# Gathers that hold 64 tokens for two heads, summed through stacked 128x64 diagonals

## The reference

```python
q = (xn @ wq).reshape(t, PEER_HEADS, PEER_D_KEY)
s1, s2 = einsum(q halves, keys1 / keys2)        # 128 scores each
v1, i1 = top_k(s1, 16); v2, i2 = top_k(s2, 16)
cs, ci = top_k(v1[..., :, None] + v2[..., None, :] flattened, 16)
expert = i1[ci // 16] * 128 + i2[ci % 16]
gate = softmax(cs)
act = gelu(einsum('td,thkd->thk', x, u_tab[expert]))
out = einsum('thk,thkd->td', gate * act, v_tab[expert])
```

## Time and profile before

| what | value |
|---|---|
| time, median of 3 executions | 4200.38 us (4197.98 to 4206.7) |
| the profiled execution, its own time | 4207.45 us |
| its span, first to last instruction | 4205.5 us |
| first gather to last `dot`, experts 0 | 527.5 to 2471.3 us |
| first gather to last `dot`, experts 1 | 2886.6 to 4183.9 us |
| gathers | 1280, 1342.31 MB |
| mean granted TensorE clock | 0.95 |

### The profile page before, as it was taken

How to read it: one execution, slowest core, us unless ns; L and a number is a source line. 1 busy time by engine, 2 the same in 40 slices (tenths; PEclk the granted TensorE clock), 3 DMA queues, 4 the chain that set the end, 5 groups by cost and what they waited for, 6 DMA issues and landing times. The chain is left out here.

```text
span 4205.5 us, 32412 instructions
## 1 busy us (share of the span) xinstructions
PE 3372.7 (80%) x9736; PEld 1548.5 (37%) x9736; DVE 2633.3 (63%) x6027; ACT 1513.4 (36%) x4394; POOL 1618.9 (38%) x1482
## 2 busy tenths in 40 slices
PE   4998887888788888788777768677887877977776
PEld 0893633333233333233222237563322322322222
DVE  3314397857857866866864444437887587587444
ACT  3210143343343343343333332333434334433333
POOL 1005044544444444444444330212444444444332
PEclk7999999999999999999999989898999999999999
DMA  8117299999999999999999951006999999999998
GB/s 353 50 61 281 95 403 394 421 421 421 417 422 416 418 413 417 418 418 418 416 405 421 422 241 60 1 33 267 394 421 421 421 419 420 421 411 415 422 421 332
DMA packets 215391, 1455.21 MB, mean 346 GB/s; under 512 B 25920, under 2 KB 25920, under 8 KB 44080
## 3 DMA queue, kind: packets, MB, share of 16 engines
q0 software_dynamic: 184704, 1342.31, 77.2%
q1 hardware_dynamic: 30400, 110.72, 7.1%
q10 hardware_dynamic: 112, 0.11, 0.0%
HBM read 1447.72 MB, written 5.34 MB: 346 GB/s over the span
## 5 line engine op out<-in xcount | busy, mean ns | idle before, releaser
L1459 PE MATMUL peer_py<-peer_ring,peer_diag 128*128 128x512 f32 x5120 | 2514.5, 626 | 617.8 <-ACT peer_diag L1389 606.4
L1342 POOL DMA_INDIRECT peer_ring<-in_uv_dram,peer_idx x1280 | 1472.0, 1150 | 1803.7 <-PE peer_py L1459 1682.8
L1559 DVE CUSTOM_DVE_ANT_0 peer_ring<-peer_ring,peer_f 128x1024 f32<-128x1024 f32 x1280 | 1555.9, 1225 | 925.3 <-DMA peer_ring<-in_uv_dram,peer_idx 915.3
L1459 PEld LDWEIGHTS peer_py<-peer_ring,peer_diag 128*128 128x128 f32 x5120 | 929.1, 195 | 2155.5 <-ACT peer_diag L1389 1324.0
L1383 ACT ACTIVATE peer_gel<-peer_u 128x1 f32<-128x1 f32 x1280 | 258.8, 202 | 1833.0 <-DVE peer_u L1559 1831.6
L1389 ACT ACTIVATE peer_diag<-ident,peer_coef 128x128 f32<-128x128 f32 x1280 | 513.8, 401 | 41.7
L1387 ACT ACTIVATE peer_coef<-peer_gel,peer_gate 128x1 f32<-128x1 f32 x1280 | 377.1, 295 | 46.3
L353 DVE TENSOR_TENSOR m_w_low<-m_w_low_plain,m_w_high 128x2048 fp32r<-128x2048 f32 x26 | 61.1, 2349 | 220.6 <-ACT m_w_high L348 220.6
L361 PE MATMUL m_ps<-m_w_high,m_aT_high 128*128 128x512 f32 x416 | 166.0, 399 | 4.4 <-DVE m_v L820 1.8
L1434 PE MATMUL peer_pb<-arena,peer_fT 128*128 128x512 f32 x320 | 164.1, 610 | 2.4 <-ACT peer_fT L1356 2.4
L361 PE MATMUL m_ps<-m_w_low,m_aT_high 128*128 128x512 f32 x416 | 163.8, 394 | 0.0
(11 more groups left out here) (194 smaller groups left out, 2400.0 us busy)
## 6 DMA issues: line engine op xcount, KB each, us to landing
mod_rows_sb<-in_ada_w_dram SPq DMA_DIRECT2D x33, 1024.0 KB, 5.0
peer_ring<-in_uv_dram,peer_idx POOLq DMA_INDIRECT x1280
arena<-in_ada_w_dram SPq DMA_DIRECT2D x15, 1024.0 KB, 16.2
m_w_low_plain<-in_ev_w_in_dram SPq DMA_DIRECT2D x12, 1024.0 KB, 5.1
arena<-in_peer_wq_dram SPq DMA_DIRECT2D x2, 4096.0 KB, 19.2
mod_rows_sb<-mod_rows SPq DMA_DIRECT2D x7, 1024.0 KB, 7.1
m_w_low_plain<-in_od_w_in_dram SPq DMA_DIRECT2D x6, 1024.0 KB, 5.2
m_w_low_plain<-in_ev_w_out_dram SPq DMA_DIRECT2D x4, 1024.0 KB, 5.1
```

Source lines behind the costliest of these rows:

```text
L1342: pool.indirect_dma_start(ring[:, n % RING], None, A["uv"], bass.IndirectOffsetOnAxis(idx[:, i % 2, hd, k:k + 1], 0)).then_inc(sem(f"lande ...
L1459: ins = pe.matmul(PY[:, i % 2, b], diag[:, n % RING], ring[:, n % RING, D + b * HALF:D + (b + 1) * HALF], start=s == 0, stop=s == TS - 1)
L1559: dve.tensor_tensor_reduce(x, x, f[:, i % 2], 1.0, 0.0, ALU.mult, ALU.add, u[:, n % RING:n % RING + 1]).then_inc(sem("dot"), 1)
```

## The change

Two slots now share two heads. Slot s belongs to pair s // 32, place s // 2 % 16 and g = s % 2, the half of the tile's tokens. Its gather brings, on partitions 0 to 63, the rows that 64 tokens (half g) have at the pair's first head, and on partitions 64 to 127 those that the same 64 tokens have at its second head. The number of gathers and their bytes are the same. For that the token rows, the indices and the gates must lie so that partition p and p + 64 hold the same token:

- `modulate` writes `plain`; ScalarE copies the half that stays (`f_kept`, at slot 14) and SyncE moves the other half (`rows_moved`) into `f[:, i % 2, g]`. `plain` also takes the place of `y`.
- SyncE moves indices (`places_moved`) and gates (`gates_moved`) by four DMAs each for a pair of heads or a batch (`spread`), one for each half of the tokens and each head of the pair. GpSimd waits for `idx_moved`, ScalarE for `gate_moved`.
- The diagonal is `stacked` times the coefficient: two 64x64 identities one above the other, 128x64. A matmul with it adds the two heads of a token. Half g = 0 goes to PSUM partitions 0 to 63, half g = 1 to 64 to 127, and `combine` takes two slots at a time, at every odd slot.
- The batches of the first tile's gates are (0,2), (2,4), (4,8) in place of (0,2), (2,5), (5,8).
- VectorE's chained waits in all stages use one semaphore; the instructions are the same. GpSimd makes `stacked` in the modulation stage (three instructions).

```diff
+def unit_of(s):
+    return s // 2 // TOPK, s // 2 % TOPK, s % 2
...
-        diag = sb("diag", [P, RING, P])
+        diag = sb("diag", [P, RING, HALF_P])
...
         @block.sync
+            def spread(i, to, of, lo, hi, name):
+                by_pair = of[:].rearrange("p (h x) k -> p h x k", x=2)
+                for g in range(2):
+                    for x in range(2):
+                        sp.dma_start(to[x * HALF_P:(x + 1) * HALF_P, i % 2, g, lo:hi],
+                                     by_pair[g * HALF_P:(g + 1) * HALF_P, lo:hi, x]).then_inc(sem(name), 16)
+            def rows_moved(i):
+                sp.wait_ge(sem("f"), i + 1)
...
+                for g in range(2):
+                    sp.dma_start(f[(1 - g) * HALF_P:(2 - g) * HALF_P, i % 2, g], plain[g * HALF_P:(g + 1) * HALF_P]
+                                 ).then_inc(sem("f_moved"), 16)
+            def places_moved(i, pair):
+                sp.wait_ge(sem("idx"), i * NH + 2 * pair + 2)
...
+                if i * PAIRS + pair:
+                    sp.wait_ge(sem("idx_moved"), MOVES * (i * PAIRS + pair))
+                spread(i, idx_at, idx, pair, pair + 1, "idx_moved")
+            def gates_moved(i, b):
+                lo, hi = gates_of(i)[b]
+                sp.wait_ge(sem("gate"), batch_ready(i, lo))
...
+                spread(i, gate_at, gate, lo // 2, hi // 2, "gate_moved")
+            for i in range(first, last + 1):
+                rows_moved(i)
+                for pair in range(PAIRS):
+                    places_moved(i, pair)
+                    for b, (lo, hi) in enumerate(gates_of(i)):
+                        if hi == 2 * pair + 2:
+                            gates_moved(i, b)
...
         @block.gpsimd
                     if k == 0:
-                        pool.wait_ge(sem("idx"), i * NH + hd + 1)
+                        pool.wait_ge(sem("idx_moved"), MOVES * (i * PAIRS + pair + 1))
                     if n >= RING:
                         pool.wait_ge(sem("slot_free"), n - RING + 1)
...
+            def f_kept(i):
+                act.wait_ge(sem("f"), i + 1)
...
+                for g in range(2):
+                    half = slice(g * HALF_P, (g + 1) * HALF_P)
+                    act.activation(f[half, i % 2, g], plain[half], ACT.Copy).then_inc(sem("f_kept"), 1)
...
-                act.activation(diag[:, n % RING], ident[:], ACT.Copy, scale=coef[:, at]).then_inc(sem("diag"), 1)
+                act.activation(diag[:, n % RING], stacked[:], ACT.Copy, scale=coef[:, at]).then_inc(sem("diag"), 1)
...
-                pe.wait_ge(sem("diag"), n + 1)
+                pe.wait_ge(sem("diag"), n + 2)
                 for b in range(2):
-                    ins = pe.matmul(PY[:, i % 2, b], diag[:, n % RING], ring[:, n % RING, D + b * HALF:D + (b + 1) * HALF],
-                                    start=s == 0, stop=s == TS - 1)
-                ins.then_inc(sem("slot_free"), 1)
+                    for g in range(2):
+                        at = (n + g) % RING
+                        ins = pe.matmul(PY[g * HALF_P:(g + 1) * HALF_P, i % 2, b], diag[:, at],
+                                        ring[:, at, D + b * HALF:D + (b + 1) * HALF], start=s == 0, stop=s == TS - 2)
+                ins.then_inc(sem("slot_free"), 2)
...
                 for s in range(TS):
-                    combine(i, s)
+                    if s % 2 == 1:
+                        combine(i, s - 1)
...
+            def plain_free(i):
+                if i > 0:
+                    dve.wait_ge(sem("fT_ps"), i)
+                    dve.wait_ge(sem("f_moved"), 32 * i)
+                    dve.wait_ge(sem("f_kept"), 2 * i)
...
+                if i > 0:
+                    dve.wait_ge(sem("idx_moved"), MOVES * ((i - 1) * PAIRS + hd // 2 + 1))
-                dve.tensor_scalar(idx[:, i % 2, hd], ef[:], float(layer * EXPERTS), None, ALU.add).then_inc(sem("idx"), 1)
+                dve.tensor_scalar(idx[:, hd], ef[:], float(layer * EXPERTS), None, ALU.add).then_inc(sem("idx"), 1)
```

More of the change, by code:

```diff
@@ L111, with group_rows @@
 GROUP_TERMS = GROUPS * TILES + 4
-def group_rows(dve, S, tag, g, row, ps, bias, gain, before):
+def group_rows(dve, S, tag, g, row, ps, bias, gain):
     for j in range(TILES):
         at = tile_rows(j)
-        dve.tensor_tensor(row[at], ps[at], bias[at, g], ALU.add).then_inc(S(tag + "_sum"), 1)
-    dve.wait_ge(S(tag + "_sum"), before + TILES)
+        linked(S, dve.tensor_tensor(row[at], ps[at], bias[at, g], ALU.add))
+    wait_links(dve, S)
     scaled = [j for j in range(TILES) if group_tile(g, j)[1] == 1]
@@ L123, in group_rows @@
         at = tile_rows(j)
-        dve.scalar_tensor_tensor(row[at], row[at], 1.0, gain[at], ALU.add, ALU.mult).then_inc(S(tag + "_sum"), 1)
-    done = before + TILES + len(scaled)
-    dve.wait_ge(S(tag + "_sum"), done)
+        linked(S, dve.scalar_tensor_tensor(row[at], row[at], 1.0, gain[at], ALU.add, ALU.mult))
+    wait_links(dve, S)
     dve.sem_inc(S(tag + "_rows"), 1)
-    return done
 def store_group(queue, mod_d, layer, g, row, sem):
@@ L1225 @@
 TS = NH * TOPK
+MOVES = 64
 PIECES = 4
@@ L1250, in next_piece, with peer_stage @@
     return None
-def peer_stage(nc, S, A, h, ident, mod_d, arena, rows, layer, t0, first, n_tiles):
+def peer_stage(nc, S, A, h, ident, stacked, mod_d, arena, rows, layer, t0, first, n_tiles):
     with ExitStack() as ctx:
@@ L1263, in peer_stage @@
         wq, keys = peer_buffers(arena)
-        f = sb("f", [P, 2, D])
+        f = sb("f", [P, 2, 2, D])
+        plain = sb("f_plain", [P, D])
         fT = sb("fT", [P, KC, P])
@@ L1283, in peer_stage @@
         ef = sb("ef", [P, TOPK])
-        idx = sb("idx", [P, 2, NH, TOPK], U32)
+        idx = sb("idx", [P, NH, TOPK], U32)
+        idx_at = sb("idx_at", [P, 2, 2, PAIRS, TOPK], U32)
         shifted = sb("shifted", [P, NH, TOPK])
@@ L1288, in peer_stage @@
         grec = sb("grec", [P, NH])
-        gate = sb("gate", [P, 2, NH, TOPK])
+        gate = sb("gate", [P, NH, TOPK])
+        gate_at = sb("gate_at", [P, 2, 2, PAIRS, TOPK])
         u = sb("u", [P, RING])
@@ L1393, in _ @@
             f_turned(first)
+            f_kept(first)
+            act.wait_ge(S("stacked"), 3)
             for part in range(2):
@@ L1408, in _ @@
                             f_turned(i + 1)
+                            f_kept(i + 1)
                         for part in range(2):
@@ L1501, in modulate @@
             def modulate(i):
-                x = f[:, i % 2]
+                x = plain[:]
                 dve.wait_ge(sem("root"), i + 1)
+                plain_free(i)
                 link(dve.reciprocal(ss[:, 3:4], ss[:, 2:3]))
@@ L1550, in normalise @@
                 link(dve.reciprocal(grec[:, lo:hi], gsum[:, lo:hi]))
-                dve.tensor_tensor(gate[:, i % 2, lo:hi], gexp[:, lo:hi],
+                if i > 0:
+                    dve.wait_ge(sem("gate_moved"), MOVES * (batch_ready(i, 0) - 1))
+                dve.tensor_tensor(gate[:, lo:hi], gexp[:, lo:hi],
                                   grec[:, lo:hi].rearrange("p (h o) -> p h o", o=1).broadcast_to([P, hi - lo, TOPK]), ALU.mult
@@ L1557, in dot @@
                 dve.wait_ge(sem(f"landed{n % RING}"), 16 * (n // RING + 1))
+                if s == 0:
+                    dve.wait_ge(sem("f_moved"), 32 * (i + 1))
+                    dve.wait_ge(sem("f_kept"), 2 * (i + 1))
                 x = ring[:, n % RING, 0:D]
[L1559 removed]
+                dve.tensor_tensor_reduce(x, x, f[:, i % 2, s % 2], 1.0, 0.0, ALU.mult, ALU.add, u[:, n % RING:n % RING + 1]).then_inc(sem("dot"), 1)
             def add_up(i):
@@ L1564, in add_up @@
                     dve.wait_ge(S("peer_gates"), 16 * rows_loads)
-                dve.tensor_tensor(y[:], PY[:, i % 2].rearrange("p b n -> p (b n)"), rows[:, kind(i - shift), 2], ALU.mult).then_inc(sem("y"), 1)
+                plain_free(min(i + 2, last + 1))
+                dve.tensor_tensor(plain[:], PY[:, i % 2].rearrange("p b n -> p (b n)"), rows[:, kind(i - shift), 2], ALU.mult).then_inc(sem("y"), 1)
                 dve.wait_ge(sem("y"), i + 1)
-                link(dve.tensor_tensor(h[:, i - shift], h[:, i - shift], y[:], ALU.add))
+                link(dve.tensor_tensor(h[:, i - shift], h[:, i - shift], plain[:], ALU.add))
             dve.wait_ge(S("peer_rows"), 16 * rows_loads)
```

87 lines of the change are left out of this document (51 added, 36 removed).

## The result

The changed kernel takes 4278.8 us (median of 4, 4267.16 to 4291.11) against 4203.54 us before: ratio 1.0178, 95% interval [1.0142, 1.0214], 75 us slower. The forecast was +58 us, with a range of its own from +30 to +83. The profiled execution is the longest of the four, with a span of 4288.8 us, 83.3 more than before.

What follows compares the result with a forecast made beforehand. The prediction took the DMA engines' gathers to bound the two expert stages. Its terms, 24.8 + 5 + 10 + 18 = 58 us on the median 4200.4, gave 4258 us, own range 4230 to 4284, stated range 4226 to 4308.

Steps and rivals of the forecast that it cites:

- The pace is set by the DMA engines: Both expert stages: they last as long as their gathers' bytes, 1280 gathers at 2.48 us, 3174 of 3241 us.
- The rival that TensorE paced the ring: Expert stages: late buffers cause 67 us and cheaper slots recover them, giving 4191 us; chance 0.05.
- the halves do not overlap: Expert stages: a pair's eight instructions take 3.6 us, the queue covers the lateness, giving 4262 us; chance 0.07.
- The start: Start of each expert stage: first gather waits for both heads and index moves, 12.4 us later, 24.8 us in all.
- Indices and gates: Index and gate moves beside gathers: about 2460 small packets a tile at 12.4 ns, 18 us over 9.5 tiles.
- each piece as dear as 512 B: Index and gate moves: 64 B pieces at 19.4 ns each would make the term about 28 us.
- The token rows: Token-row moves inside SBUF: 1.24 us a tile at the gathers' rate, 10 us for eight tiles; bounds 0 to 20.
- The hole and the pairs: First tile of each stage, near slot 42: freeing in pairs queues one gather fewer, 2.5 us a stage, 5 us.
- about five gathers queued: Gather ring: pairs free the even buffer 2.5 to 3 us later, leaving five gathers, 12 us cover, costed at nothing.
- Halves and clock: TensorE's sum for a pair: halves run together in four rounds, about 1.8 us at full clock; no gain booked.
- its rival: Expert stages: TensorE's clock falls to 1.2 GHz, costing 8 us in each of eight tiles, 64 us; chance 0.08.
- The sum: Whole kernel: start, hole, token rows, indices and gates add up to 58 us, own range 30 to 83.

Runs made afterwards that it cites:

- b_half: Kernel before, with the second matmul of each slot left out except at a tile's first and last slot; ratio 1.0012 to the kernel before.
- b_start: Kernel before, with GpSimd's first gather of a pair of heads waiting until both heads are routed; ratio 1.0032 to the kernel before.
- a_one_half: Changed kernel, with both token halves summed into the lower 64 array columns except at a tile's first and last pair; ratio 1.0206 to the kernel before.
- b_rows_one: Kernel before, plus one unread move of token rows per tile, 128 partitions in one transfer; ratio 1.0020 to the kernel before.
- b_pair: Kernel before, with the sum done for two slots at a time and both buffers freed together, diagonals still 128x128; ratio 1.0037 to the kernel before.
- b_all_moves: Kernel before, plus unread row, index and gate moves, GpSimd's wait for moved indices and buffers freed in pairs, without the 128x64 halves; ratio 1.0207 to the kernel before.
- b_rows: Kernel before, plus two unread moves of 64 token rows of 4 KB for each tile; ratio 1.0059 to the kernel before.
- b_small: Kernel before, plus the change's index and gate moves on SyncE into tiles nobody reads; ratio 1.0034 to the kernel before.

## Why the forecast held, point by point

- *The pace is set by the DMA engines.* Shown by b_half, and by b_start, where a later first gather is paid in full. The rival that TensorE paced the ring is out for the kernel before. In the changed kernel it is out only because the halves run side by side: a_one_half, with pairs of 3.65 us, is short of gathers in places (share 0.97). The prediction priced this case (*the halves do not overlap*) at under 4 us and held that the queue would cover the rest. The step of 5.4 us that it reckoned with is measured as 5.49; what failed is that the queue covers it: it cost 23 us of the phases, and 12 in the time.
- *The start*: forecast 24.8 us, measured 12.9 + 11.9 = 24.8. The moves' issues were dearer (2.38 us for four, against 1.7), so GpSimd starts 3.8 us after head 1's index is written and not 3.4; the sum is right to within what the two stages differ by. The terms that the prediction names (3.1 us behind 536.51) give 539.6 and not 539.9, so 24.2 us; that it meets the measured sum to the tenth is chance.
- *Indices and gates*: 18 us from 12.4 ns a packet; measured alone 15.4 us, 10.1 ns. The estimate that the prediction tied to the Trainium skill's statement on transfers below 512 B ("DMA: Bandwidth & Descriptors", Specifications), each piece as dear as 512 B, would have given about 28; the run speaks against so high a price for pieces of 64 B. The upper end of 25 us that the prediction's own range uses for this term is worked out nowhere, and its check of the packet count leaves 384 over (1280 gathers of 128 rows and 16 signals are 184320, not 184704).
- *The token rows*: this is the mis-sized term. Forecast 10 us from their bytes, bound 20; measured 27.5 alone. The bytes were right (b_rows_one 8.5), the step that failed was that a move costs its bytes at the gathers' rate whatever its partitions. The same page, Rules for kernel authors, advises one transfer of 128 partitions in place of two to disjoint halves, because they serialize; this case agrees with the advice and is dearer than serializing explains. That it is the halves of SBUF into which each transfer writes at one time is my reading, not shown: b_rows_one changes the number of transfers and the partitions of each together, and neither one transfer of 64 partitions nor one of 128 that crosses the halves was tried.
- *The hole and the pairs*: forecast 5 us and "about five gathers queued"; b_pair alone costs 14.3, all of it in the first tile of each stage, half of it outside the hole. The cover of five gathers, costed at nothing, held in the later tiles and not in the first; which of the first tile's waits makes the other half was not separated. In the changed kernel the hole costs 10.6 us of gathers (309 GB/s over 40 us) where it cost 6.7.
- *Halves and clock*: four rounds, 1.94 us, as forecast; the clock fell as its rival said, to a mean of 0.79, but it brought none of its 64 us: with the clock low in part of its pairs the changed kernel's phases equal, within 1 us, those of b_all_moves, whose mean clock is 0.938. The rival wanted the low clock in the query steps, and of these only the first has it: from 940 to 960 us (the row is shown with a_one_half) it is 1.00 and the DMA engines are full, as the argument against the rival had it. The low clock falls into pairs with slack around them.
- *The sum.* 24.8 + 45.4 + 1.7 = 71.9 of the 75 us. One by one the parts of the phases make 58.7; together 46.7. They overlap by some 12 us, probably because an engine held up by a move is one that another cause would have left idle, but which pair of edits overlaps was not separated. The forecast of 33 us for these parts was short by 12, and that would have been 26 without the overlap: the rows were 17 short, the pairs 9. That the total lies well inside the range is in part luck, since nothing in the prediction foresaw the overlap that took 12 us off. The forecast was right in its way and in which terms it named, and too low in two of them.

## What to carry to other kernels

Where a queue of large gathers is full from end to end, count what an edit adds to the DMA engines, not what it takes from TensorE. Move a tile across all 128 partitions in one transfer; two transfers of 64 beside gathers cost nearly three times their bytes. Buffers freed in pairs cost nothing where the queue is long and are dear where the ring already runs dry, here in the first tile of a stage; judge the cover there and not by the queue's mean length. And a wait in the first tile of a stage that is out of step by six slots is worth looking for before any larger edit.

## What the runs showed of the hardware that I had not expected

- Two transfers of 64 partitions x 4 KB beside gathers of 128 x 8 KB cost 3.4 us a tile (b_rows), one of 128 partitions 1.1 us (b_rows_one), with a busy share of 1.0 in both.
- A piece of 64 bytes inside SBUF, beside full gathers, costs 10.1 ns of a DMA engine (b_small), not much more than the 8.0 ns of the small packets of the earlier trace rows, loads from HBM with nothing beside them.
- In the changed kernel TensorE's granted clock changes level from pair to pair (mean 0.53 in a pair of 3.63 us, 1.00 in the next of 1.94 us); in a_one_half the pairs in the same stretch take 3.65 us each, and the mean over the span is 0.936.
